# Two transformer blocks in one Trainium2 kernel: who makes the low parts of the weights

## The chip, the core and the metric

The kernel runs on one core of a Trainium2 chip. Its time is the device time of one execution in microseconds, as the median of several runs. Five engines work side by side and meet only through semaphores: TensorE (PE) multiplies, VectorE (DVE), ScalarE (ACT) and GpSimd (POOL) work on tiles elementwise, and SyncE (SP) issues the loads. Each engine works through its own instructions in the order in which they are written, and a wait holds up all that stands behind it.

## The reference

Two decoder blocks on 256 tokens of width 2048, in float32, one after the other:

```
h = x + mixer_block(rms_norm(x, norm_mix_w), w_in, ...)          # HGRN2 scan, 8 heads + banded attention, 16 heads
h = h + square(relu(rms_norm(h, norm_mlp_w) @ w_up)) @ w_down    # d_ff 8192
h = rms_norm(h, norm_final_w)
x = mixer_block_2(h, ...)                                        # gMLP, 8 groups + neighbourhood attention, 16 heads
x = conv_ffn(x, norm_ffn, w_up, conv_k, conv_b, w_down)          # silu(gate) * value, conv of width 3, d_ff 5504
return rms_norm(x, norm_final)
```

Both mixers project the input into heads and gates (w_in), join two branches with w_branch under sigmoid gates, and project back with w_out. Nearly all of the arithmetic is in the large weight products.

## The kernel before, in words

Activations lie transposed, with channels on the partitions and the 256 tokens along the free axis. To keep nearly float32 accuracy with the faster fp32r products, each operand is split into a high part (rounded to fp32r) and a low part (what the rounding left). A product is hi*hi + hi*lo + lo*hi. For this, an activation tile holds its high part in columns 0 to 255 and its low part in columns 256 to 511. The high part of a weight k-tile multiplies all 512 columns (`L401`), its low part only the first 256 (`L403`).

The weights come in 960 blocks, mostly 1024 x 128 (eight k-tiles, 128 x 1024 in SBUF, 512 KB). Every block passes through four hands:

- SyncE loads it into one of five buffers `w_raw` (`L337`), when the low parts of the block four before it are done (`L335`, `L336`).
- ScalarE rounds all 1024 columns into `w_hi` (`round_block`, `L737`), when the data is there and TensorE has used block b.
- VectorE makes columns 0 to 511 of `w_lo` = `w_raw` - `w_hi` (`low_part`, `L1157`), and GpSimd makes columns 512 to 1023 of it with the same instruction (`low_part`, `L1049`), each when `hi_done` says so.
- TensorE waits for both low parts (`L395`, `L396`) and issues the 16 products of the block.

`LEAD` is 4: at step b of a phase the elementwise engines prepare block b+4. The other work is put by hand into the same steps, behind the preparation of the block. `round_block` and `low_part` are the first calls of a step on each engine. Then ScalarE copies the second half of the finished PSUM bank into `cross` (`L742`), VectorE adds the bank's halves (`tile_sum`, `L1163`), which frees the bank (`acc_free`), and multiplies by the row scale (`scaled_tile`, `L1169`, or `L1393`, `L1534`). Most VectorE instructions are followed by a wait for their own semaphore (`mark`, `link`).

The phases: heads1 (8 rounds of 22 blocks: the projections of one scan head and two attention heads, with decay products, softmax and scan between them), branch1, out1, ffn1first, ffn1 (3 rounds of 64 blocks), ffn1last, gmv, heads2 (8 rounds of 16), branch2, out2, ffn2first, ffn2 (2 rounds of 96) and ffn2last. In heads1 the steps 1 to 7 carry the chain of the forget gate: sigmoid and scaling of q (`L1250`), of f (`L1256`, `L1257`), the logarithm on ScalarE (`L816`), its transposition on TensorE (`L461`), the gate of the output (`L1262`) and the low part of the logarithm (`L1265`, `lg_lo`). The steps 8 to 16 carry the decays: `L1280` on VectorE and `L1087` on GpSimd multiply the same exponentials `HS` with q and k, `L1289`, `L1292` and `L1294` mask and reduce their products. In softmax, `L1228` and `L1229` divide by the sums. In the branches `L1352` makes the low part of the merged tile. In ffn2, `L1520` and `L1521` are the convolution's taps.

GpSimd's other work is small: `L1087` in heads1, and the sums of squares for the norms (`L1054`, `L1072`, `L1121`, `L1137`) in the start, out1, ffn1last, out2 and ffn2last. It also sets `ones` in four pieces, each of which counts `lo_pool` up by one, so that the first waits (`CREDIT` = 4) are met.

Of the kernel before, what the change touches and what calls it, by code (L numbers as in the profile page):

```python
# [6 lines left out]
F32 = mybir.dt.float32  # L7
# [29 lines left out]
LEAD = 4  # L37
# [129 lines left out]
def two_blocks(  # L167
# [8 lines left out]
    with ExitStack() as ctx:  # L176
# [87 lines left out]


        landed = [sem(f"landed{s}") for s in range(SLOTS)]
        hi_done, lo_dve, lo_pool, w_used = sem("hi_done"), sem("lo_dve"), sem("lo_pool"), sem("w_used")
        acc_free, cross_ready = sem("acc_free"), sem("cross_ready")
        dve_step, act_step = sem("dve_step"), sem("act_step")
        x_in, c_in, v_in = sem("x_in"), sem("c_in"), sem("v_in")  # L270
# [57 lines left out]
        def _(sp):  # L328
            def load(name, p, i, b):
                kt, ncols = p.shapes.get(b, (KB, P))  # L330
                s = p.slot(b)
                tensor, offset, ap = weight_source(name, i, b)
                freed = p.block(i, b) - REUSE + 1 + CREDIT

                sp.wait_ge(lo_dve, freed)  # L335
                sp.wait_ge(lo_pool, freed)  # L336
                sp.dma_start(w_raw[s][:, 0:kt * ncols].rearrange("p (k n) -> p k n", k=kt),  # L337
                             bass.AP(tensor=tensor, offset=offset, ap=ap)).then_inc(landed[s], 16)

# [46 lines left out]
        def _(pe):  # L386
            def products(p, i, b, bank, X, k0, first, last, nk=KB, col=0, width=P, operand=None):


                s = p.slot(b)  # L390
                hi = w_hi[s][:, 0:nk * width].rearrange("p (k n) -> p k n", k=nk)
                lo = w_lo[s][:, 0:nk * width].rearrange("p (k n) -> p k n", k=nk)
                if col == 0:

                    pe.wait_ge(lo_dve, p.block(i, b) + 1 + CREDIT)  # L395
                    pe.wait_ge(lo_pool, p.block(i, b) + 1 + CREDIT)  # L396
                for k in range(nk):
                    if operand is not None:

                        pe.wait_ge(operand[0], operand[1] + k0 + k + 1)  # L400
                    nc.tensor.matmul(bank[:, :], hi[:, k, col:col + P], X[:, k0 + k, :],  # L401
                                     start=first and k == 0, stop=False, skip_group_check=True)
                    done = nc.tensor.matmul(bank[:, 0:T], lo[:, k, col:col + P], X[:, k0 + k, 0:T],  # L403
                                            start=False, stop=last and k == nk - 1, skip_group_check=True)
                if col + P == width:
                    done.then_inc(w_used, 1)
# [8 lines left out]


            pe.wait_ge(c_in, 16)
            pe.wait_ge(x_in, 16 * NT)
            xn = Gf[:, 0:NT * D].rearrange("p (a n) -> p a n", a=NT)
            banks = [psE, psA]  # L420
# [619 lines left out]

        @block.gpsimd
        def _(pool):
            def low_part(p, i, b):
                c = b + LEAD
                if p is last_phase and c >= p.blocks:
                    return
                s, n = p.slot(c), (p.size(c) if c < p.blocks else BLOCK)
                pool.wait_ge(hi_done, p.block(i, c) + 1)
                nc.gpsimd.tensor_tensor(w_lo[s][:, n // 2:n], w_raw[s][:, n // 2:n], w_hi[s][:, n // 2:n].bitcast(F32),  # L1049
                                        ALU.subtract).then_inc(lo_pool, 1)  # L1050

            def add_square(n):
                pool.wait_ge(sq_ready, n + 1)
                nc.gpsimd.tensor_tensor(sqacc[:, 0, :], sqacc[:, 0, :], sqb[:, 0, :], ALU.add).then_inc(sq_added, 1)  # L1054
# [5 lines left out]
                pool.wait_ge(S("sums_cleared"), cleared[0])  # L1060

            cleared = [0]
            for n in range(CREDIT):
                nc.gpsimd.memset(ones[:, n * 32:(n + 1) * 32], 1.0).then_inc(lo_pool, 1)
            clear_sums()
            for b in range(LEAD):
                pool.wait_ge(hi_done, b + 1)
                nc.gpsimd.tensor_tensor(w_lo[b][:, BLOCK // 2:], w_raw[b][:, BLOCK // 2:], w_hi[b][:, BLOCK // 2:].bitcast(F32),
                                        ALU.subtract).then_inc(lo_pool, 1)
            for j in range(KD):  # L1070
                pool.wait_ge(sq_ready, j + 1)
                nc.gpsimd.tensor_tensor(sqacc[:, 0, :], sqacc[:, 0, :], sqb[:, j % 2, :], ALU.add).then_inc(sq_added, 1)  # L1072
# [2 lines left out]
            p = ph["heads1"]  # L1075
            with pool.Fori(0, p.iters) as i:
                for b in range(p.blocks):
                    low_part(p, i, b)
                    if b in (8, 10, 12, 14):
                        k = (b - 8) // 2  # L1080
                        pool.wait_ge(S("decay_exp"), i * 4 + k + 1)
                        if k == 0:
                            pool.wait_ge(S("g_ready"), i + 1)
                        else:
                            pool.wait_ge(S("pairs_full"), i * 4 + k)
                        kk = wk(1)[:, (k // 2) * P:(k // 2 + 1) * P].rearrange("p (a t) -> p a t", a=1)
                        nc.gpsimd.tensor_tensor(HS[:, 2, :, :], HS[:, 0, :, :], kk.to_broadcast([P, 4, P]), ALU.mult)\  # L1087
                          .then_inc(S("kE_ready"), 1)

            def plain(name):  # L1090
                p = ph[name]
                if p.iters == 1:
                    for b in range(p.blocks):
                        low_part(p, 0, b)
                else:
                    with pool.Fori(0, p.iters) as i:
                        for b in range(p.blocks):
                            low_part(p, i, b)

            def out_projection(name, n0):  # L1100
                p = ph[name]
                with pool.Fori(0, p.iters) as i:
                    for b in range(p.blocks):
                        low_part(p, i, b)
                        if b % 2:
                            add_square(i * 8 + (n0 * KD + b // 2))

            plain("branch1")
            pool.wait_ge(stat_done, 1)
            clear_sums()  # L1110
            out_projection("out1", 1)
            plain("ffn1first")
            plain("ffn1")
            pool.wait_ge(stat_done, 2)
            clear_sums()
            p = ph["ffn1last"]
            for b in range(p.blocks):
                low_part(p, 0, b)
                add_square(2 * KD + b)
                pool.wait_ge(sq2_ready, b + 1)  # L1120
                nc.gpsimd.tensor_tensor(sqacc[:, 1, :], sqacc[:, 1, :], sqb[:, 1, :], ALU.add).then_inc(sq2_added, 1)  # L1121
                pool.wait_ge(sq2_added, b + 1)
            plain("gmv")
            plain("heads2")
            plain("branch2")
            pool.wait_ge(stat_done, 4)
            clear_sums()
            out_projection("out2", 3)
            plain("ffn2first")
            plain("ffn2")  # L1130
            pool.wait_ge(stat_done, 5)
            clear_sums()
            p = ph["ffn2last"]
            for b in range(p.blocks):
                low_part(p, 0, b)
                pool.wait_ge(S("sqf_ready"), b + 1)
                nc.gpsimd.tensor_tensor(sqacc[:, 0, :], sqacc[:, 0, :], wk(6 + b % 2), ALU.add).then_inc(S("sqf_added"), 1)  # L1137
                pool.wait_ge(S("sqf_added"), b + 1)
# [3 lines left out]
        def _(dve):  # L1142
# [8 lines left out]
            def low_part(p, i, b):  # L1151
                c = b + LEAD
                if p is last_phase and c >= p.blocks:
                    return
                s, n = p.slot(c), (p.size(c) if c < p.blocks else BLOCK)
                dve.wait_ge(hi_done, p.block(i, c) + 1)
                V.tensor_tensor(w_lo[s][:, 0:n // 2], w_raw[s][:, 0:n // 2], w_hi[s][:, 0:n // 2].bitcast(F32),  # L1157
                                ALU.subtract).then_inc(lo_dve, 1)

            def tile_sum(p, i, c, b, t, bank, dst):  # L1160
# [16 lines left out]
            dve.wait_ge(acc_free, TILE_CREDIT)  # L1177
            for b in range(LEAD):
                dve.wait_ge(hi_done, b + 1)
                V.tensor_tensor(w_lo[b][:, 0:BLOCK // 2], w_raw[b][:, 0:BLOCK // 2], w_hi[b][:, 0:BLOCK // 2].bitcast(F32),  # L1180
                                ALU.subtract).then_inc(lo_dve, 1)
            banks = (psE, psA)

# [428 lines left out]
```

## Time and profile before

| | |
|---|---|
| runs of the kernel before | 3140.42, 3141.75, 3149.58 us; median 3141.75 |
| span of the profiled execution | 3139.2 us |
| TensorE busy | 2927.3 us, 93% |
| VectorE busy | 2169.0 us, 69% |
| GpSimd busy | 1680.3 us, 54% |
| ScalarE busy | 1515.2 us, 48% |
| DMA | 519.81 MB, mean 166 GB/s |

The profiled execution has its span, from the first to the last instruction, and no time of its own beside the runs; the median of the runs lies 2.5 us above the span. Busy is the time in which an engine has an instruction at work, waits inside of that instruction included. The matmuls' ends are modelled, so a busy TensorE may still be one that runs below its peak; its idle time is better read from the waits. A line number behind L is that of the kernel's text. "A <- B" in a row of waits says that A's engine sat idle until B was done.

### The profile page before, as it was taken

The numbers are of one execution on the slowest core, as the hardware profiler recorded it, in microseconds if no ns is written. First come the engines' busy times: TensorE is split into PE (matmuls) and PEld (weight loads), VectorE is DVE, ScalarE is ACT, GpSimd is POOL, SyncE is SP. The second block draws the span as 40 slices with busy tenths as digits, with TensorE's granted clock in tenths as the row PEclk, the third lists the DMA queues.
The fourth block names the chain that finished last, engine by engine and source line by source line (L and its number), as shares of the span: only waits on it lengthen the run. The fifth ranks groups of instructions, "written<-read, shape, count | busy, mean of one in ns | idle before, by whom it ended". The sixth has DMA issues, their size and how long they took to land.

```text
span 3139.2 us, 53753 instructions
## 1 busy us (share of the span) xinstructions
PE 2927.3 (93%) x16379; PEld 2496.7 (80%) x16379; DVE 2169.0 (69%) x3324; ACT 1515.2 (48%) x2293; POOL 1680.3 (54%) x1105
## 2 busy tenths in 40 slices
PE   5999999989999999999988999899899999999997
PEld 4777777778788888888876777777787788888886
DVE  5777777777568655556577666656747888878885
ACT  5544555556444444444463444445555444444454
POOL 4444445445655666656673445444374455555554
PEclk9999999999999999999999999999999999999998
DMA  5455555545556666666754555565565566666664
GB/s 160 144 146 145 145 145 146 146 140 165 172 173 177 191 190 186 185 183 192 202 148 135 151 155 162 144 163 154 155 188 156 166 182 183 189 177 190 187 182 123
DMA packets 1016035, 519.81 MB, mean 166 GB/s; under 512 B 28980, under 2 KB 1014700, under 8 KB 1015596
## 3 DMA queue, kind: packets, MB, share of 16 engines
q1 hardware_dynamic: 1014032, 513.90, 57.5%
q10 hardware_dynamic: 1820, 3.65, 0.3%
q8 instruction: 93, 1.52, 0.2%
q14 instruction: 90, 0.74, 0.1%
HBM read 515.35 MB, written 2.13 MB: 165 GB/s over the span
## 4 chain that ended last, share of the span: by engine, by line
PE 54%; DVE 27%; issue 9%; ACT 7%; DVEq 1%; DMA 0%; ACTq 0%; SPq 0%; POOL 0%; POOLq 0%
PE acc L401 24%; PE acc L403 12%; DVE w_lo L1157 6%; PE psX L401 5%; PE psT L401 5%; ACT w_hi L737 4%; PE psX L403 2%; PE psT L403 2%; DVE work L1163 2%; DVE work L1534 2%; DVE hT L1362 1%; DVE hT L1361 1%; DVE work L1521 1%; DVE work L1520 1%; DVE HS L1280 1%
## 5 line engine op out<-in xcount | busy, mean ns | idle before, releaser
L1049 POOL TENSOR_TENSOR w_lo<-w_raw,w_hi 128x512 fp32r<-128x512 f32 (+1 forms) x960 | 1548.2, 1625 | 1385.5 <-ACT w_hi L737 1381.5
L1157 DVE TENSOR_TENSOR w_lo<-w_raw,w_hi 128x512 fp32r<-128x512 f32 (+1 forms) x960 | 906.6, 950 | 688.6 <-ACT w_hi L737 634.6
L737 ACT ACTIVATE w_hi<-w_raw 128x1024 fp32r<-128x1024 f32 (+1 forms) x960 | 995.4, 1050 | 601.1 <-PE acc L403 467.4
L401 PE MATMUL acc<-XU,w_hi 128*128 128x512 f32 x3488 | 1256.7, 402 | 26.6 <-DVE work L1163 18.7
L403 PE MATMUL acc<-XU,w_lo 128*128 128x256 f32 x3488 | 983.6, 282 | 0.0
L401 PEld LDWEIGHTS acc<-XU,w_hi 128*128 128x128 f32 x3488 | 662.0, 190 | 195.7 <-DVE w_lo L1157 18.5
L401 PE MATMUL acc<-XY,w_hi 128*128 128x512 f32 x2112 | 768.6, 405 | 44.6 <-DVE work L1163 18.4
L403 PEld LDWEIGHTS acc<-XU,w_lo 128*128 128x128 f32 x3488 | 665.5, 191 | 1.1
L403 PE MATMUL acc<-XY,w_lo 128*128 128x256 f32 x2112 | 598.9, 284 | 0.0
L401 PEld LDWEIGHTS acc<-XY,w_hi 128*128 128x128 f32 x2112 | 404.0, 191 | 151.1 <-DVE w_lo L1157 23.6
L403 PEld LDWEIGHTS acc<-XY,w_lo 128*128 128x128 f32 x2112 | 407.2, 193 | 0.1
L401 PE MATMUL psT<-XY,w_hi 128*128 128x512 f32 x632 | 226.4, 398 | 14.2 <-issue 9.4
L401 PE MATMUL psX<-XY,w_hi 128*128 128x512 f32 x632 | 225.6, 397 | 2.0 <-DVE work L1163 1.6
L403 PE MATMUL psT<-XY,w_lo 128*128 128x256 f32 x632 | 177.3, 281 | 0.0
L403 PE MATMUL psX<-XY,w_lo 128*128 128x256 f32 x632 | 177.2, 280 | 0.0
L401 PEld LDWEIGHTS psT<-XY,w_hi 128*128 128x128 f32 x632 | 118.6, 188 | 45.5 <-issue 11.7
L1002 ACT ACTIVATE work<-work,convc 128x256 f32<-128x256 f32 x86 | 51.8, 603 | 190.8 <-DVE work L1534 190.7
L401 PEld LDWEIGHTS psX<-XY,w_hi 128*128 128x128 f32 x632 | 118.6, 188 | 31.3 <-DVE w_lo L1157 1.7
L401 PE MATMUL psX<-XU,w_hi 128*128 128x512 f32 x352 | 125.5, 396 | 1.9 <-DVE work L1163 1.1
L401 PE MATMUL psT<-XU,w_hi 128*128 128x512 f32 x352 | 125.1, 395 | 0.4 <-POOL w_lo L1049 0.4
L1163 DVE TENSOR_TENSOR work<-acc,cross 128x256 f32<-128x256 f32 x290 | 120.7, 416 | 5.5 <-ACT cross L742 5.2
L403 PEld LDWEIGHTS psT<-XY,w_lo 128*128 128x128 f32 x632 | 119.4, 189 | 0.0
(250 smaller groups left out, 2993.5 us busy)
## 6 DMA issues: line engine op xcount, KB each, us to landing
w_raw<-in_w_in SPq DMA_DIRECT2D x320, 512.0 KB, 3.9
w_raw<-in_w_up SPq DMA_DIRECT2D x300, 512.0 KB, 4.4
w_raw<-in_w_down SPq DMA_DIRECT2D x208, 512.0 KB, 4.3
w_raw<-in_w_out SPq DMA_DIRECT2D x64, 512.0 KB, 3.9
w_raw<-in_w_branch SPq DMA_DIRECT2D x32, 512.0 KB, 3.8
w_raw<-in_w_branch_a SPq DMA_DIRECT2D x16, 512.0 KB, 3.8
w_raw<-in_w_branch_b SPq DMA_DIRECT2D x16, 512.0 KB, 3.8
bias<-in_rel_bias SPq DMA_DIRECT2D x8, 384.0 KB, 5.1
```

What stands on the lines that cost most here:

```text
L401: nc.tensor.matmul(bank[:, :], hi[:, k, col:col + P], X[:, k0 + k, :], start=first and k == 0, stop=False, skip_group_check=True)
L403: done = nc.tensor.matmul(bank[:, 0:T], lo[:, k, col:col + P], X[:, k0 + k, 0:T], start=False, stop=last and k == nk - 1, skip_group_check ...
L737: act.activation(w_hi[s][:, 0:n], w_raw[s][:, 0:n], ACT.Copy).then_inc(hi_done, 1)
L1002: act.activation(wk(2 + u.value), work[:, u.value, 0:T], ACT.Identity, scale=convc[:, 0, ds(ch, 1)], bias=convc[:, 3, ds(ch, 1)]).then_inc ...
L1049: nc.gpsimd.tensor_tensor(w_lo[s][:, n // 2:n], w_raw[s][:, n // 2:n], w_hi[s][:, n // 2:n].bitcast(F32), ALU.subtract).then_inc(lo_pool, 1)
L1157: V.tensor_tensor(w_lo[s][:, 0:n // 2], w_raw[s][:, 0:n // 2], w_hi[s][:, 0:n // 2].bitcast(F32), ALU.subtract).then_inc(lo_dve, 1)
L1163: mark(V.tensor_tensor(dst, bank[:, 0:T], cross[:, c % 2, :], ALU.add), acc_free, p.tile(i, t) + 1 + TILE_CREDIT)
L1280: mark(V.tensor_tensor(HS[:, 1, :, :], HS[:, 0, :, :], q.to_broadcast([P, 4, P]), ALU.mult), S("qE_ready"), i * 4 + k + 1)
L1361: link(V.tensor_tensor(h, bank[:, 0:T].rearrange("p (a t) -> p a t", a=1), h, ALU.add))
L1362: mark(V.tensor_tensor(h, bank[:, T:2 * T].rearrange("p (a t) -> p a t", a=1), h, ALU.add), acc_free, p.tile(i, t) + 1 + TILE_CREDIT)
L1520: link(V.scalar_tensor_tensor(y, z, convc[:, 1, ds(ch, 1)], y, ALU.mult, ALU.add))
L1534: mark(V.tensor_tensor(z, z, rs[:, :], ALU.mult), S("conv_z"), (made(name, i, s.group) + s.t) * 2 + s.value + 1)
```

## The change

The low part of a block is made by one VectorE instruction on all 1024 columns. GpSimd's half, its semaphore `lo_pool` and all waits for it are gone; GpSimd keeps its other work. `ones` is set by one instruction, and TensorE waits for it once, at its start.

```diff
@@ SyncE, load
                 sp.wait_ge(lo_dve, freed)
-                sp.wait_ge(lo_pool, freed)
@@ TensorE, products
                     pe.wait_ge(lo_dve, p.block(i, b) + 1 + CREDIT)
-                    pe.wait_ge(lo_pool, p.block(i, b) + 1 + CREDIT)
@@ TensorE, start
             pe.wait_ge(c_in, 16)
+            pe.wait_ge(S("ones_set"), 1)
             pe.wait_ge(x_in, 16 * NT)
@@ GpSimd
-            def low_part(p, i, b):
-                c = b + LEAD
-                if p is last_phase and c >= p.blocks:
-                    return
-                s, n = p.slot(c), (p.size(c) if c < p.blocks else BLOCK)
-                pool.wait_ge(hi_done, p.block(i, c) + 1)
-                nc.gpsimd.tensor_tensor(w_lo[s][:, n // 2:n], w_raw[s][:, n // 2:n], w_hi[s][:, n // 2:n].bitcast(F32),
-                                        ALU.subtract).then_inc(lo_pool, 1)
...
-            for n in range(CREDIT):
-                nc.gpsimd.memset(ones[:, n * 32:(n + 1) * 32], 1.0).then_inc(lo_pool, 1)
+            nc.gpsimd.memset(ones[:, :], 1.0).then_inc(S("ones_set"), 1)
...
@@ VectorE, low_part
                 dve.wait_ge(hi_done, p.block(i, c) + 1)
-                V.tensor_tensor(w_lo[s][:, 0:n // 2], w_raw[s][:, 0:n // 2], w_hi[s][:, 0:n // 2].bitcast(F32),
+                V.tensor_tensor(w_lo[s][:, 0:n], w_raw[s][:, 0:n], w_hi[s][:, 0:n].bitcast(F32),
                                 ALU.subtract).then_inc(lo_dve, 1)
@@ VectorE, start
-                V.tensor_tensor(w_lo[b][:, 0:BLOCK // 2], w_raw[b][:, 0:BLOCK // 2], w_hi[b][:, 0:BLOCK // 2].bitcast(F32),
+                V.tensor_tensor(w_lo[b][:, :], w_raw[b][:, :], w_hi[b][:, :].bitcast(F32),
                                 ALU.subtract).then_inc(lo_dve, 1)
```

In GpSimd's program the calls of `low_part` go with it, also in the phases in which it did nothing else.

## Rows read from the trace of the kernel before

In rows 2 and 10 the columns are: the stretch and its length; busy us of PE, PEld, DVE, ACT and POOL, each with its count; TensorE's granted clock; the DMA share; GB/s.

**Rows 1.** The chain that ended last: share of the span by engine.
```profile
PE 54%; DVE 27%; issue 9%; ACT 7%; DVEq 1%; DMA 0%; ACTq 0%; SPq 0%; POOL 0%; POOLq 0%
```
**Rows 2.** Stretches: heads1, branch1, ffn1first, ffn1, ffn1last, gmv, heads2, ffn2first, ffn2.
```profile
43.40:697.80 654.40, 603.38 (x3426) 508.84 (x3425) 471.10 (x673) 329.10 (x521) 316.45 (x208) 0.99 0.50 144
697.80:802.10 104.30, 93.57 (x514) 79.63 (x513) 79.13 (x129) 65.26 (x121) 51.45 (x32) 0.98 0.55 159
...
893.60:1038.50 144.90, 137.79 (x772) 119.59 (x771) 111.53 (x143) 63.34 (x86) 71.54 (x50) 0.98 0.60 174
1038.50:1577.20 538.70, 536.43 (x3075) 469.99 (x3074) 319.23 (x577) 231.33 (x288) 338.03 (x193) 1.00 0.67 190
1577.20:1629.80 52.60, 45.99 (x258) 38.94 (x256) 48.10 (x64) 33.65 (x59) 48.76 (x45) 0.97 0.53 155
1629.80:1709.30 79.50, 61.89 (x300) 49.62 (x301) 55.22 (x74) 33.58 (x50) 30.85 (x23) 0.89 0.48 131
1709.30:2162.70 453.40, 418.40 (x2306) 344.59 (x2304) 282.50 (x428) 208.90 (x329) 213.22 (x127) 0.98 0.56 152
...
2358.80:2517.80 159.00, 144.60 (x803) 122.29 (x803) 125.62 (x187) 78.41 (x119) 73.59 (x53) 1.00 0.55 159
2517.80:3072.70 554.90, 545.64 (x3074) 471.79 (x3072) 449.33 (x652) 272.26 (x391) 307.89 (x193) 1.00 0.65 186
```
**Rows 3.** VectorE: a group (busy, mean ns), two lines (ns minimum/median/maximum).
```profile
L1157 DVE TENSOR_TENSOR w_lo<-w_raw,w_hi 128x512 fp32r<-128x512 f32 x952 | 898.9, 950 | 688.3 <-ACT w_hi L737 634.6 <-issue 7.3 <-DVE hT L1362 1.7
...
L1157 DVE TENSOR_TENSOR w_lo<-w_raw,w_hi x960: 557/693/1836, 50.5 to 3114.3; 128x512 fp32r<-128x512 f32 x192
...
L1534 DVE TENSOR_TENSOR work<-work,rs x86: 426/1065/1073, 2372.1 to 3067.5; 128x256 f32<-128x256 f32 x86
```
**Rows 4.** GpSimd's groups: its half of the low parts.
```profile
L1049 POOL TENSOR_TENSOR w_lo<-w_raw,w_hi 128x512 fp32r<-128x512 f32 x952 | 1539.9, 1630 | 1359.7 <-ACT w_hi L737 1355.7
```
**Rows 5.** Order of time in one round of heads1, VectorE: start, duration.
```profile
302.83 1.52 DVE L1250 SCALAR_TENSOR_TENSOR work<-work 128x256 f32<-128x256 f32 x1
304.47 1.58 DVE L1157 TENSOR_TENSOR w_lo<-w_raw,w_hi 128x512 fp32r<-128x512 f32 x1
...
308.95 1.38 DVE L1256 TENSOR_SCALAR work<-work,small 128x256 f32<-128x256 f32 x1
...
317.07 1.50 DVE L1262 SCALAR_TENSOR_TENSOR work<-work,small 128x256 f32<-128x256 f32 x1
...
320.18 0.41 DVE L1265 TENSOR_TENSOR lg_lo<-psT,lg_hi 128x256 fp32r<-128x256 f32 x1
```
**Rows 6.** VectorE's widest instruction, 1024 columns: ns minimum/median/maximum.
```profile
L1561 DVE TENSOR_SCALAR G<-G,small x2: 746/749/752, 3130.9 to 3131.5; 128x1024 f32<-128x1024 f32 x2
```
**Rows 7.** Waits of the weight loads in heads1: total, times, longest.
```profile
PEld psT L461 <- ACT work L816: 24.7, 8, 3.4
```
**Rows 8.** Order of time in heads1: the decay multiplies of VectorE and GpSimd.
```profile
346.47 1.78 DVE L1280 TENSOR_TENSOR HS<-HS,work 128x512 f32<-128x512 f32 x1
...
347.66 1.55 POOL L1087 TENSOR_TENSOR HS<-HS,work 128x512 f32<-128x512 f32 x1
```
**Rows 9.** heads2: a wait of the weight loads, and a group of the softmax.
```profile
PEld acc L401 <- DVE w_lo L1157: 14.0, 8, 1.8
...
L1228 DVE TENSOR_SCALAR probs<-probs,soft 128x256 f32<-128x256 f32 x24 | 27.7, 1153 | 0.9
```
**Rows 10.** The stretch behind the softmax's wait in one round of heads2.
```profile
1927.00:1933.00 6.00, 5.98 (x25) 4.60 (x25) 3.19 (x6) 1.06 (x1) 0.81 (x2) 0.72 0.82 216
```
**Rows 11.** Order of time in branch1's second round.
```profile
789.89 1.25 DVE L1352 TENSOR_TENSOR XU<-work,XU 128x256 f32 x1 [0.18 <-DVE work L1347]
```
**Rows 12.** Waits of the weight loads in gmv.
```profile
PEld acc L401 <- DVE G L1163: 11.5, 5, 6.7
```
**Rows 13.** Order of time in ffn2: one period of six blocks, begin and end.
```profile
2600.43 1.07 DVE L1534 TENSOR_TENSOR work<-work,rs 128x256 f32<-128x256 f32 x1
...
2617.39 1.07 DVE L1534 TENSOR_TENSOR work<-work,rs 128x256 f32<-128x256 f32 x1
```

More of the change, by code:

```diff
@@ L266, in two_blocks @@
         landed = [sem(f"landed{s}") for s in range(SLOTS)]
-        hi_done, lo_dve, lo_pool, w_used = sem("hi_done"), sem("lo_dve"), sem("lo_pool"), sem("w_used")
+        hi_done, lo_dve, w_used = sem("hi_done"), sem("lo_dve"), sem("w_used")
         acc_free, cross_ready = sem("acc_free"), sem("cross_ready")
@@ L1062, in _ @@
             cleared = [0]
-            for n in range(CREDIT):
-                nc.gpsimd.memset(ones[:, n * 32:(n + 1) * 32], 1.0).then_inc(lo_pool, 1)
+            nc.gpsimd.memset(ones[:, :], 1.0).then_inc(S("ones_set"), 1)
             clear_sums()
[L1066 to L1069, printed above, removed]
             for j in range(KD):
@@ L1077, in _ @@
                 for b in range(p.blocks):
-                    low_part(p, i, b)
                     if b in (8, 10, 12, 14):
@@ L1088, in _ @@
                           .then_inc(S("kE_ready"), 1)
[L1090 to L1098, printed above, removed]
             def out_projection(name, n0):
@@ L1103, in out_projection @@
                     for b in range(p.blocks):
-                        low_part(p, i, b)
                         if b % 2:
                             add_square(i * 8 + (n0 * KD + b // 2))
-            plain("branch1")
             pool.wait_ge(stat_done, 1)
@@ L1111, in _ @@
             out_projection("out1", 1)
-            plain("ffn1first")
-            plain("ffn1")
             pool.wait_ge(stat_done, 2)
@@ L1117, in _ @@
             for b in range(p.blocks):
-                low_part(p, 0, b)
                 add_square(2 * KD + b)
@@ L1122, in _ @@
                 pool.wait_ge(sq2_added, b + 1)
-            plain("gmv")
-            plain("heads2")
-            plain("branch2")
             pool.wait_ge(stat_done, 4)
@@ L1128, in _ @@
             out_projection("out2", 3)
-            plain("ffn2first")
-            plain("ffn2")
             pool.wait_ge(stat_done, 5)
@@ L1134, in _ @@
             for b in range(p.blocks):
-                low_part(p, 0, b)
                 pool.wait_ge(S("sqf_ready"), b + 1)
```

## The prediction

> **What bounds the kernel now.** I read the chain of waits first, then the stretches, then the groups of instructions, and at last the order of time inside one head. The chain shows TensorE with 54% of the span and VectorE with 27% [rows 1]. So TensorE sets the pace, and where it does not, VectorE's chain does. The stretches say where [rows 2]. TensorE multiplies 960 weight blocks of eight k-tiles. In ffn1 a block costs 538.7 / 192 = 2.81 us and the engine is busy all the time; I take that as the floor. Everywhere else a block costs more: heads1 3.72 (654.4 / 176), branch1 3.26, ffn1first 3.02, ffn1last 3.29, gmv 4.97, heads2 3.54, ffn2first 3.18, ffn2 2.89. Part of the excess is the small products between blocks. The rest is waiting on VectorE, mostly on what comes out of a long chain ScalarE, VectorE, ScalarE.
>
> Why those chains are long stands in the groups. VectorE's half of a low part takes 0.95 us in the mean and 0.69 in the median; `L1534`, the same operation on 256 columns, takes 0.43 at its shortest and 1.07 in its median [rows 3]. GpSimd's half takes 1.63 us in the mean [rows 4]. In order of time: VectorE's half runs first, GpSimd starts just behind it, and the next VectorE instruction on SBUF alone takes 1.52 (`L1250`), 1.38 (`L1256`) or 1.50 (`L1262`), while `L1265`, which reads PSUM, takes 0.41 [rows 5]. So the two engines shut each other out for whole instructions. The Trainium skill has this in SBUF — State Buffer, "Who interferes with whom": a VectorE instruction with two SBUF inputs and a GpSimd instruction that reads SBUF exclude each other for the whole of whichever started first. The trace agrees (1.07 against 0.43).
>
> **The price of the new low part.** No instruction of that form and width is in the trace. From below, the only VectorE instruction on 1024 columns takes 0.75, with one input [rows 6]. From above, two halves in a row are 2 x 0.69 = 1.38 by the undisturbed half, or 2 x 0.95 = 1.90 by the mean. I take the line through the undisturbed 256 and 512 columns, 0.43 and 0.69 [rows 3]: 0.26 to 0.27 for each 256, hence 0.69 + 2 x 0.267 = 1.23. So each low part costs VectorE 1.23 - 0.69 = 0.54 more than a free half, 0.28 more than the mean half (960 x 0.28 = 269 us busy), and w_lo is complete after 1.23 instead of the 1.75 that GpSimd's slower half usually needs. What is freed is the 0.6 to 1.1 us on each instruction that was shut out. Cases run from a VectorE chain with one low part and one shut-out instruction (gain 0.54 lost, 0.64 to 1.1 won) to one with three low parts and none (1.6 lost). The sum is made stretch by stretch.
>
> Edits at nothing: one memset of `ones` for four and TensorE's wait for it lie under the loads of x (the first transposes wait for these anyway; uncovered, below 0.5 us). SyncE's loads and TensorE's blocks lose a wait on GpSimd; they now hang on VectorE's alone, which comes 0.5 earlier where VectorE is on time. Four blocks of lead (11 us) cover the rest.
>
> **heads1, 8 rounds, -20 us.** The gate of the first half is `psT L461`, 24.7 us of waiting, and behind it lg_lo, which ends at 320.59 [rows 7, 5]. I replay the chain with 1.23 and 0.42, and 0.35 for one-input ones on 256 columns (an estimate from the 0.75 for 1024). Link hq to hf: low +0.54, `L1250` -1.10, low 1.58 to 1.23 -0.35: -0.9. Link to Ln: two lows +1.08, `L1256` -1.03, and its successor `L1257`, shut out the same way, -0.91: -0.9. Link to lg_lo: +0.54 -1.08 (`L1262`) -0.33: -0.9. The two lows at the head of the round give up to 0.8 more, of which I count 0.3: -3.0 a round. Second half (b 10 to 17): eight low parts, six short ones +0.6 each, two long ones -0.4 each, against three `L1280` (1.78 to 0.69 in one [rows 8], 1.50 in the others), `L1294` twice (-1.0, -0.5) and `L1228` (-0.7). If VectorE goes first at `L1280` this is -0.6; if GpSimd's multiply `L1087` does [rows 8] (about 1.1 alone), VectorE waits for it and it is +1.1. It will often be asked for while VectorE's longer low part still runs, so I take +0.5. The same section of the skill says that whoever starts first decides, which speaks against the change here; by it alone this half is +1.1 and heads1 -15. Sum: 8 x (-3.0 + 0.5) = -20, bounds -29 and -10.
>
> **heads2, 8 rounds, -23 us.** No GpSimd work is left here. TensorE waits 14.0 us, 1.75 a round, where the row names w_lo; the instruction behind is the sum of tile 5 that frees the bank [rows 9], and before it for the softmax (1.5). On that chain stand three free lows (+0.54 each), `L1476` (1.53 to 0.56), four `L1228`/`L1229` (1.15 in the mean [rows 9], to 0.35; -3.2) and a low of 1.55 to 1.23. That is 1.6 - 1.0 - 3.2 - 0.3 = -2.9 of chain; of the 3.2 that TensorE waits there I give back 2.3 a round, 18 in all. The wait drops the granted clock: 0.72 in the 6 us behind one [rows 10], a good half of them at the lower level of 1.2 GHz; a block takes 4.3 instead of 2.7. In five of eight rounds I see this; -5 for it. Bounds -28 and -10.
>
> **branch1 and branch2 with the start of out1 and out2, -13.** A pair of blocks costs VectorE 6.40 in the second round against TensorE's 5.6. Of this `L1352` is shut out, 1.25 [rows 11]. New: +0.61 for the short low, -0.83, -0.26: 5.9. Over 16 pairs VectorE falls behind by about 5 instead of 13 us, less than the lead for most of the way; the waits at b 8 to 14 (2.9) go and the last one (5.9) shrinks to about 3. -6 each, -1 for the clock. Bounds -4 and -20.
>
> **ffn1first, -9.** VectorE's cycle of two blocks is 6.27; new 5.3, below TensorE's 5.55. The stretch lies 144.9 - 48 x 2.81 = 10 above the floor [rows 2], nearly all of it waiting on this cycle; 9 of it goes. Bounds -5 and -10.
>
> **ffn1last and gmv, -11.** VectorE's cycle in ffn1last is 3.40 a block (a shut-out low of 1.67); new 2.65 alone, up to 3.24 with GpSimd's square sums between. The end of the chain, on which gmv's first sums hang, comes 4.5 earlier. In gmv the cycle of a pair falls from 6.8 to 5.9: -5.5 of the 11.5 [rows 12], and 1 at the end. Bounds -5 and -18.
>
> **ffn2first -5, ffn2 -2, ffn1 and the ends 0.** In ffn2first's mixed part VectorE and ScalarE are in step, 15.0 a round of five blocks. Deltas: +0.61 +0.60 for lows, -0.50 -0.46 for long ones, -0.64 for `L1534`: 14.6, 8 rounds, -3.3; 2 more at its head. In ffn2 the period is 2617.39 - 2600.43 = 16.96 for six blocks [rows 13]. VectorE's own chain there comes to 16.96 now and 16.6 after, so no new bound appears, but the margin is only 0.3. ffn1's VectorE is busy 1.7 of 2.8 us a block and 2.1 after; hidden. In ffn2last the low stands before the output copies: +1.
>
> Sum: -20 -23 -13 -9 -11 -5 -2 = -83, by rounding with the +1. From the profiled 3139.2 this gives 3056; the median of the runs (3141.75) is 2.5 above the span, so **3059 us**. The terms' bounds give 3010 to 3105.
>
> **Rivals.**
> *The lockstep eats it (3104).* Chains cross ScalarE, whose round (1.05) and copies stay, and each new low stands at the head of a step, before the sum that frees the bank. Then heads1 gives 8, heads2 10, the branches 7, ffn1first 7, gmv 6, the rest nothing: -38. For it: VectorE's total busy time stays about what it is (269 us more for the lows, about 320 us less elsewhere). Against: the gates I name all stand behind a shut-out instruction.
> *More than counted (3029).* A block in ffn2 costs 2.89 and in ffn1 2.81 [rows 2] with TensorE nearly always busy in both; if the slow manner goes with VectorE's lateness, 192 x 0.08 = 15 us go there and as much in the other stretches. For: it is in the stretches with the fuller VectorE. Against: one of ffn1's three rounds has it too.
> *Slower: VectorE becomes the bound (3337).* If the long durations are not GpSimd's doing, a full low part costs 2 x 0.95 = 1.90, 0.67 above my price. Then ffn2's period is 16.6 + 6 x 0.67 = 20.6, +3.7 on 32 periods, +118 against now; heads1 and heads2 lose half of 304 x 0.67, 102; the branches 43, ffn2first 27. With the -83 that is about +195, some of the rest counted in. It decides from a low part of 1.4 us on, where the loss on all of these equals 83. Against: the PSUM reader at 0.41 amid its slow neighbours [rows 5]. Nor does the change fail to do what it says: the row of GpSimd's w_lo must vanish.
>
> **How the numbers follow.** Forecast 0.60 (its own range 3030 to 3092), lockstep 0.20, more 0.12, slower 0.07, no change 0.01. The range 3015 to 3125 holds the first three nearly whole. A difference under 0.3% can't be told from none here. Faster by more 0.88 (the first three less 0.04 for the lockstep case's weak end), within 0.05, slower 0.07.
>
> **What would show it.** `L1534`, `L1250`, `L1169` at 0.42 to 0.43 throughout and the new w_lo group at 1.23 with little spread; VectorE busy within 80 us of 2169. The wait of `psT L461` for ScalarE from 3.1 a round to below 1; `psT L531` in heads2 without a wait; heads1's round 81.8 to about 79.3, heads2's 56.7 to about 53.8; ffn1 at 538 unchanged; ffn2 within 5 us. The forecast is wrong if a low part takes over 1.4, if ffn2's period rises above 17, or if heads1's round stays, which would put the gate on ScalarE.

## The result, and the profile after

The changed kernel is faster. Four runs took 3024.90 to 3035.66 us, median 3031.61, against a median of 3145.45 for four runs of the kernel before. The ratio is 0.9631, with a 95% interval from 0.9611 to 0.9651. On another chip it was 0.9652 (0.9627 to 0.9676). The forecast was 3059 and the range 3015 to 3125, so mechanism and side were right and the size was short: 83 us forecast, 114 measured between the medians, 105 between the two spans. The measured time lies at the edge of the forecast's own range (3030 to 3092) and nearer to the 3029 of the rival "more than counted" than to 3059; what became of that rival stands below.

The profiled execution has a span of 3033.9 us. This is the page's busy time, each engine with its share and its count, and the chain of waits by engine, which answers to [rows 1]:

```profile
PE 2901.6 (96%) x16379; PEld 2480.3 (82%) x16379; DVE 2170.2 (72%) x3324; ACT 1524.8 (50%) x2293; POOL 133.9 (4%) x138
...
PE 65%; DVE 17%; issue 9%; ACT 7%; DVEq 1%; DMA 0%; ACTq 0%; SPq 0%; POOL 0%; POOLq 0%
```

VectorE took over GpSimd's half of the low parts and is busy for as long as before (2170.2 for 2169.0 us). Its share of the chain fell from 27% to 17%. The groups and lines of VectorE show why. They answer to [rows 3] and to the first row of [rows 5]; the first row gives busy time and mean ns, the others minimum, median and maximum:

```profile
L1120 DVE TENSOR_TENSOR w_lo<-w_raw,w_hi 128x1024 fp32r<-128x1024 f32 x952 | 1164.8, 1228 | 591.9 <-ACT w_hi L736 531.0 <-issue 17.6 <-DVE hT L1325 1.2
...
L1497 DVE TENSOR_TENSOR work<-work,rs x86: 424/426/429, 2288.8 to 2961.2; 128x256 f32<-128x256 f32 x86
...
L1213 DVE SCALAR_TENSOR_TENSOR work<-work x8: 418/418/422, 56.2 to 606.5; 128x256 f32<-128x256 f32 x8
...
L1243 DVE TENSOR_TENSOR HS<-HS,work x32: 691/1582/1591, 74.9 to 647.3; 128x512 f32<-128x512 f32 x32
```

The whole low part takes 1.228 us, where the line through two widths gave 1.23. The row scale of ffn2 (`L1534`, now `L1497`) had a median of 1065 ns and now has 426, with a maximum of 429. `L1243`, the old `L1280`, is still shut out, 24 of 32 times and 21 us in all: GpSimd's multiply is the one large thing GpSimd kept beside it. Beside GpSimd's sums of squares at the start and in ffn1last, `L1149` takes 753 ns in the mean for 473 at its shortest, `L1330` 720 for 484, and six low parts are longer too, about 11 us together.

The stretches, in the order of [rows 2] and with its columns: heads1, branch1, ffn1first, ffn1, ffn1last, gmv, heads2, ffn2first, ffn2.

```profile
42.50:672.10 629.60, 594.95 (x3425) 503.22 (x3424) 456.81 (x673) 331.25 (x521) 42.23 (x33) 1.00 0.53 150
672.10:772.80 100.70, 91.72 (x514) 79.32 (x513) 77.45 (x129) 66.28 (x122) 0.00 (x0) 0.97 0.56 164
...
865.40:1002.20 136.80, 136.30 (x773) 118.02 (x772) 96.05 (x144) 63.76 (x86) 1.26 (x2) 1.00 0.64 186
1002.20:1547.10 544.90, 543.23 (x3074) 470.54 (x3073) 385.25 (x577) 230.79 (x288) 0.00 (x0) 1.00 0.65 188
1547.10:1595.50 48.40, 45.48 (x259) 39.21 (x257) 45.41 (x65) 34.04 (x60) 33.98 (x28) 1.00 0.60 175
1595.50:1665.60 70.10, 61.56 (x300) 50.56 (x301) 45.31 (x74) 34.22 (x50) 4.62 (x5) 0.88 0.52 141
1665.60:2088.40 422.80, 409.16 (x2306) 338.86 (x2304) 270.07 (x428) 208.08 (x329) 0.00 (x0) 1.00 0.60 164
...
2276.50:2423.50 147.00, 143.18 (x804) 122.62 (x803) 115.33 (x189) 78.78 (x120) 1.27 (x2) 1.00 0.59 172
2423.50:2965.50 542.00, 538.32 (x3074) 467.95 (x3072) 423.21 (x650) 277.58 (x391) 0.00 (x0) 1.00 0.66 190
```

heads2 gives most (453.4 to 422.8), then heads1 (654.4 to 629.6), ffn1last with gmv (132.1 to 118.5), ffn2 (554.9 to 542.0) and ffn2first (159.0 to 147.0). One of these stretches got longer: ffn1, 538.7 to 544.9, though TensorE is busy in nearly all of it in both traces (536.4 and 543.2 us).

The waits of TensorE's weight loads in heads1 answer to [rows 7]: total, times, longest.

```profile
PEld psA L495 <- DVE HS L1252: 25.9, 8, 3.3
PEld psE L472 <- DVE lg_lo L1228: 10.9, 8, 1.4
PEld psT L460 <- ACT work L815: 5.3, 7, 1.1
```

The wait for the logarithm fell from 24.7 to 5.3. The wait for the masked products (`HS`) rose from 16.5 to 25.9 and is now the largest.

### The profile page after: what moved, and what is told of

Read it like the earlier page. It is cut to its first block, busy times and chain, and to the rows that moved or that the text cites. A ratio compares the mean times of both kernels' runs of the same rounds, so it can differ in the third digit from the quotient of the medians.

```text
span 3033.9 us, 50114 instructions
## 1 busy us (share of the span) xinstructions
PE 2901.6 (96%) x16379; PEld 2480.3 (82%) x16379; DVE 2170.2 (72%) x3324; ACT 1524.8 (50%) x2293; POOL 133.9 (4%) x138
## 3 DMA queue, kind: packets, MB, share of 16 engines
q8 instruction: 90, 1.47, 0.2%
## 4 chain that ended last, share of the span: by engine, by line
PE 65%; DVE 17%; issue 9%; ACT 7%; DVEq 1%; DMA 0%; ACTq 0%; SPq 0%; POOL 0%; POOLq 0%
PE acc L399 29%; PE acc L401 14%; PE psT L399 6%; PE psX L399 6%; DVE w_lo L1120 5%; ACT w_hi L736 4%; PE psX L401 3%; PE psT L401 3%; DVE work L1126 1%; DVE probs L1184 1%; DVE HS L1243 1%; ACT probs L782 1%; DVE soft L1185 1%; DVE work L1132 1%; DVE HS L1252 1%
## 5 line engine op out<-in xcount | busy, mean ns | idle before, releaser
L1120 DVE TENSOR_TENSOR w_lo<-w_raw,w_hi 128x1024 fp32r<-128x1024 f32 (+1 forms) x960 | 1171.9, 1226 | 592.1 <-ACT w_hi L736 531.0
L399 PE MATMUL acc<-XU,w_hi 128*128 128x512 f32 x3488 | 1243.7, 399 | 6.7 <-DVE work L1126 6.0
L401 PEld LDWEIGHTS psX<-XY,w_lo 128*128 128x128 f32 x632 | 119.2, 189 | 0.0
L1044 POOL TENSOR_TENSOR sqacc<-sqacc,sqb 128x256 f32<-128x256 f32 x48 | 44.7, 932 | 1562.5 <-ACT sqb L878 1562.0
```

The costliest lines, as they stand in the source:

```text
L1120: V.tensor_tensor(w_lo[s][:, 0:n], w_raw[s][:, 0:n], w_hi[s][:, 0:n].bitcast(F32), ALU.subtract).then_inc(lo_dve, 1)
```

## The experiments

Three questions were open. How much is the shutting out worth, and how much of it does VectorE's longer instruction give back? Does the longer instruction cost because of its length or because of its place? And what moved ffn1 and ffn2? Each version was timed beside the kernel before, which took 3148.3 us in the median beside the first four, 3146.9 beside the next four and 3148.7 beside the last, on another chip.

**The same kernel once more.**

> The changed kernel itself once more, on the chip of the next ones. Theory A (two manners of TensorE): in a stretch without a stall TensorE keeps one of two cadences, 346.7 or 352 ns for a pair of products, and which one is decided anew at each stall; then ffn1 (545.0 us, all slow in the first trace) and ffn2 (542.0, first round slow, second fast) can differ by up to 10 us each from trace to trace of the same program, while heads1 and heads2 stay within 5. Rival B: the cadence belongs to the program; then the same rounds are slow again and all stretches agree within 2 us.

Measured: 3039.34 us, ratio 0.9652. The two traces of one program disagree where theory A said. These windows have the same clock (1.00) and no idle TensorE, first in the trace after, then in the second trace:

```profile
1190.00:1360.00 170.00, 170.00 (x964) 147.51 (x963) 121.55 (x181) 72.00 (x90) 0.00 (x0) 1.00 0.64 185
2700.00:2900.00 200.00, 200.00 (x1156) 174.83 (x1155) 156.03 (x241) 103.30 (x145) 0.00 (x0) 1.00 0.66 190
```

```profile
1190.00:1360.00 170.00, 170.00 (x982) 149.90 (x982) 121.74 (x182) 73.06 (x91) 0.00 (x0) 1.00 0.66 188
2700.00:2900.00 200.00, 200.00 (x1133) 173.49 (x1132) 153.51 (x236) 101.19 (x142) 0.00 (x0) 1.00 0.65 187
```

In 170 us TensorE issued 964 products in one trace and 982 in the other, and in ffn2 it is the other way round (1156 and 1133). That is 1.9 to 2.0%. Worked out from the starts of the products, a pair takes 346.7 or 353.3 ns in the mean of a round (waits left out), and a whole round of ffn1 or ffn2 keeps one of the two. ffn1 took 545.0 and 541.9, ffn2 542.0 and 546.8; heads1 629.6 and 632.2. So the cadence is not the program's, and B falls. That it is decided anew at each stall, as A has it, no run shows. In the second trace block 19 of two rounds of heads1 ran at the lower level of the clock (1.2 for 2.4 GHz) and took 5.3 and 5.0 us for 3.9; in the first trace none did.

**Half of each low part left out.** GpSimd's half is gone and VectorE does not take it over; those columns stay at zero from the start.

```diff
-                V.tensor_tensor(w_lo[s][:, 0:n], w_raw[s][:, 0:n], w_hi[s][:, 0:n].bitcast(F32),
+                V.tensor_tensor(w_lo[s][:, 0:n // 2], w_raw[s][:, 0:n // 2], w_hi[s][:, 0:n // 2].bitcast(F32),
... the same at VectorE's start, and GpSimd clears the other columns once
```

> Leaves out the second half of each low part (its columns are zero from the start), so neither engine makes it: VectorE does 0.69 a block, GpSimd nothing. Theory A: the gain of the change is the shutting out that went (about -140 to -150 us by itself), of which VectorE's longer low part (1.23 for 0.69) gives back 30 to 45: about 2990 us, ratio 0.952, most of the difference to the change in heads1 and heads2, which have 8 and 3 low parts on the chains that gate TensorE. Rival B (VectorE's own work costs nothing, it is all hidden): 3030 as the change itself, ratio 0.963.

Measured: 2934.05 us, ratio 0.9319 (0.9299 to 0.9340). Against the kernel before this is nearly the shutting out alone, with VectorE's work unchanged: 3148.3 - 2934.1 = 214 us. TensorE's own waits for GpSimd's half, which went with it, were 3.7 us in all in the trace before, of which this is the largest row:

```profile
PE acc L401 <- POOL w_lo L1049: 2.6, 3, 1.9
```

Against the change on the same chip it is 3039.3 - 2934.1 = 105 us, which is what the longer low part gives back. Theory A had the right signs and both sizes too small, B falls. TensorE has hardly an idle moment in heads1 (589.2 us) and heads2 (407.5). The zeros are not what makes it fast there: a later version with all columns made has the same two lengths.

**Two halves on VectorE.**

```diff
-                V.tensor_tensor(w_lo[s][:, 0:n], w_raw[s][:, 0:n], w_hi[s][:, 0:n].bitcast(F32),
-                                ALU.subtract).then_inc(lo_dve, 1)
+                V.tensor_tensor(w_lo[s][:, 0:n // 2], w_raw[s][:, 0:n // 2], w_hi[s][:, 0:n // 2].bitcast(F32), ALU.subtract)
+                V.tensor_tensor(w_lo[s][:, n // 2:n], w_raw[s][:, n // 2:n], w_hi[s][:, n // 2:n].bitcast(F32),
+                                ALU.subtract).then_inc(lo_dve, 1)
```

> The change with VectorE making the low part in two instructions of half a block. Theory A: 2 x 0.69 = 1.38 for 1.23 in trains of two; VectorE busy +140 us, and 0.15 more for each low part on a gating chain: heads1 +8, heads2 +4, branches and gmv +4, in all about 3047, ratio 0.969. Rival B (the width of the instruction is what brings the gain): above 3080.

Measured: 3069.17 us, ratio 0.9729 (0.9686 to 0.9772), between the two theories: 30 us above the change on this chip, where A has 15 and B 48 or more (3047 and 3080 against 3031.6). The halves take 0.692 and 0.701 us. The four runs range from 3047.9 to 3081.4 us, and the trace is that of the slowest. In it the loss is largest in heads1, 655.9 for 629.6: 3.3 us a round. Its waits for the logarithm, lg_lo and `HS` grew by 0.3, 0.1 and 0.4 us a round, and in all eight rounds block 19 ran at the lower level of the clock and took 5.4 to 6.3 us for 3.9; that costs 2.2 a round, two thirds of the loss. The second and third of these blocks:

```profile
191.50:198.00 6.50, 5.75 (x19) 4.98 (x20) 5.92 (x13) 1.20 (x2) 0.00 (x0) 0.50 0.37 102
273.50:280.00 6.50, 5.74 (x19) 4.96 (x20) 5.92 (x13) 1.22 (x2) 0.00 (x0) 0.50 0.36 105
```

What puts the clock down there is not settled, and two rounds of the change's second trace show it too. So one instruction for two is worth about 30 us here in the median, from 9 to 42 by the run; in the traced run a good part of it comes by way of the clock.

**GpSimd kept beside the whole low part.** GpSimd makes its half once more, behind VectorE's.

```diff
 # from the kernel before; VectorE makes w_lo[s][:, 0:n]
-                pool.wait_ge(hi_done, p.block(i, c) + 1)
+                pool.wait_ge(lo_dve, p.block(i, c) + 1 + CREDIT)
                 nc.gpsimd.tensor_tensor(w_lo[s][:, n // 2:n], w_raw[s][:, n // 2:n], w_hi[s][:, n // 2:n].bitcast(F32),
... the same for the first four blocks
```

> VectorE makes the whole low part as in the change, and GpSimd makes its half once more behind it, so its instruction follows VectorE's as in the kernel before and can shut out the next one on SBUF. Theory A: the shut-out waits come back (0.6 to 1.1 us on the instruction behind each low part) on top of 1.23: ffn2's period of six blocks rises from 16.7 to about 20, heads1 and heads2 by 8 and 4 us a round against the change, the sum about 3300, slower than before; L1534's kind is back at 1.07 to 1.7. Rival B (the waits of VectorE had another cause than GpSimd's reads): within 1% of the change.

Measured: 3402.10 us, ratio 1.0813 (1.0789 to 1.0837). A's direction holds, its size was 100 us too small. The groups of VectorE and GpSimd in this version (busy, mean ns):

```profile
L1157 DVE TENSOR_TENSOR w_lo<-w_raw,w_hi 128x1024 fp32r<-128x1024 f32 x952 | 1300.7, 1378 | 396.5 <-ACT w_hi L737 320.1 <-issue 14.8 <-DVE hT L1362 1.4
L1534 DVE TENSOR_TENSOR work<-work,rs 128x256 f32<-128x256 f32 x86 | 98.9, 1150 | 2.9
...
L1049 POOL TENSOR_TENSOR w_lo<-w_raw,w_hi 128x512 fp32r<-128x512 f32 x952 | 1413.1, 1490 | 1746.1 <-DVE w_lo L1157 1744.1
```

`L1534` is back at 1.15, from 0.43 where GpSimd makes no low parts. Order of time in ffn2 shows one after the other what GpSimd's instruction does to those with SBUF inputs (1.38, 1.28) and to those that read PSUM (0.42):

```profile
2561.01 1.38 DVE L1521 SCALAR_TENSOR_TENSOR work<-work,convc 128x256 f32<-128x256 f32 x1
2563.89 1.23 DVE L1157 TENSOR_TENSOR w_lo<-w_raw,w_hi 128x1024 fp32r<-128x1024 f32 x1 [1.50 <-ACT w_hi L737]
2565.03 0.42 DVE L1163 TENSOR_TENSOR work<-acc,cross 128x256 f32<-128x256 f32 x1
2565.49 1.28 DVE L1534 TENSOR_TENSOR work<-work,rs 128x256 f32<-128x256 f32 x1
```

Four versions now stand in a square. TensorE waits for GpSimd's late half in the last one, so its corner holds that too.

| us, ratio | VectorE makes half (0.69) | VectorE makes all (1.23) |
|---|---|---|
| GpSimd makes a half | 3148.3, 1 | 3402.1, 1.0813 |
| GpSimd makes none | 2934.1, 0.9319 | 3039.3, 0.9652 |

GpSimd's half costs 214 us beside a half and 363 beside the whole. VectorE's second half costs 105 without GpSimd and 254 with it. The change goes over the diagonal: -214 + 105 = -109.

**The low part last in the step, heads1 and heads2.**

```diff
                 for b in range(p.blocks):
-                    low_part(p, i, b)
                     t = b // 2
...
                         low_of_attention(1, i, XY)
+                    low_part(p, i, b)
```

> The change with VectorE's low part at the end of each step instead of its head, in heads1 and heads2 only. Leaving half of each low part out brought 40 us in heads1 and 15 in heads2 against the change. Theory A (a low part costs because it stands ahead of the tile sum and the chain's multiplies in the same step, not because VectorE is full): the waits of TensorE for lg_lo, HS and the keys shrink from 5.2 us a heads1 round and 2.1 a heads2 round to below 2 and 1, heads1 about 605 us for 630, heads2 about 412 for 423, in all near 3000, ratio 0.953. Rival B (VectorE's total work in the chain counts, wherever it stands, because it is without a gap there): within 8 us of the change, ratio 0.964.

Measured: 2973.60 us, ratio 0.9445 (0.9429 to 0.9460). heads1 588.6 and heads2 405.8 us, what the version with half of the work left out had (589.2 and 407.5). So the same instructions on the same engine cost nothing that the trace shows there once they stand behind the chain's own. B falls, and A was too cautious: the waits for the logarithm, lg_lo and `HS` are gone, not smaller. The largest wait of the weight loads left in that stretch is that of the start:

```profile
PEld psS L412 <- POOL sqacc L1057: 4.7, 1, 4.7
```

**GpSimd's multiply on VectorE.**

```diff
... GpSimd's part in heads1 is gone
+                        kk = wk(1)[:, (k // 2) * P:(k // 2 + 1) * P].rearrange("p (a t) -> p a t", a=1)
+                        mark(V.tensor_tensor(HS[:, 2, :, :], HS[:, 0, :, :], kk.to_broadcast([P, 4, P]), ALU.mult),
+                             S("kE_ready"), i * 4 + k + 1)
```

> The change with GpSimd's multiply of the decays with k (1.10 us, and 1.58 for VectorE's own multiply behind it where 0.69 is free) made by VectorE. Theory A (GpSimd goes first and shuts VectorE out for about 0.9 a time): VectorE's pair costs 2 x 0.69 = 1.38 for 1.58, three times on the chain to HS, so the 3.2 us wait of each heads1 round shrinks by some 0.5: -2 to -6 us in all. Rival B (the added 0.69 is on the chain in full): heads1 +15 to +20 us.

Measured: 3028.39 us, ratio 0.9617 (0.9593 to 0.9642), not to be told from the change. heads1 took 631.5 us for 629.6. B's 15 to 20 us did not come. A's 2 to 6 can't be seen in the time, but they are in the waits: that for `HS` fell from 25.9 to 23.3, and a round of heads1 with block 19 at the full clock takes 78.1 to 78.2 us (the first apart) for 78.4 to 78.6. In three rounds block 19 ran at the lower level, which takes it away again. VectorE does twice 0.69 where it did 0.69 and waited 0.89.

```profile
PEld psA L495 <- DVE HS L1241: 23.3, 8, 3.0
```

**The low part last everywhere, and with the multiply on VectorE.**

```diff
 # in branches, out_projection, ffn1, gmv, heads2 and ffn2 alike
-                        low_part(p, i, b)
...
+                        low_part(p, i, b)
```

> The low part at the end of VectorE's step in every phase. Theory A: as the version in heads1 and heads2 alone, and besides gmv -5, ffn2first -5, ffn2last -2, ffn1last -2, branches -3: about 2985 us, ratio 0.949. Rival B: in steps that wait for ScalarE or TensorE at their end the low part of block b+4 comes too late, TensorE waits for w_lo, and the stretches with a full VectorE (branches, ffn2first) get longer by 5 to 10 us each.

> Both: low part last in every phase and the multiply with k on VectorE. With theory A of both, 2 to 6 us below the version with the low part last; with rival B of the multiply 15 above it. If the chain to HS no longer gates, the multiply changes nothing (within 3 us).

Measured: 2943.45 us, ratio 0.9344 (0.9328 to 0.9361), and with the multiply 2952.67, 0.9369 (0.9344 to 0.9395). The first is the fastest complete version, 3% below the change and 42 us below A's 2985. Beyond heads1 and heads2 it took gmv from 70.2 to 64.7, ffn2first from 147.0 to 140.5 and ffn2last from 68.3 to 61.8 us. No stretch got longer by more than the cadence does, so B falls here too. The multiply brings nothing that can be told apart: the medians differ by 9 us, the intervals overlap, and heads1 takes 589.2 for 587.6. The stretch of heads1 shows TensorE busy in 587.18 of 587.60 us:

```profile
42.50:630.10 587.60, 587.18 (x3420) 502.87 (x3421) 442.39 (x676) 333.62 (x520) 48.17 (x34) 1.00 0.57 160
```

**The kernel before with VectorE's half last in the step.**

> The kernel before, both engines making their halves, with VectorE's half moved to the end of its step in every phase (GpSimd's stays at the head of its own). Theory A (the place on VectorE takes the low part off the chains, but GpSimd's half still shuts out the multiply behind each tile sum): about half of what the move brought to the changed kernel, near 3090 us, ratio 0.982, L1534's kind still near 1.0 us. Rival B (the place alone was the matter, who makes the half is not): as the changed kernel with the low part last, 2943, ratio 0.935.

Measured: 3008.60 us, ratio 0.9554 (0.9538 to 0.9570), between A and B. The place alone is worth 140 us in the kernel before, more than the change itself, and more than the 96 us that the same move brought the changed kernel (3039.3 to 2943.5), where A had expected half of it. heads1 and heads2 give 101 of the 133 us between the spans (654.4 to 599.9 and 453.4 to 406.7), and TensorE no longer waits for the logarithm, lg_lo or `HS` there. GpSimd's half on top costs 3008.6 - 2943.5 = 65 us, a third of the 214 it cost with the low part first. The groups of this version (busy, mean ns) show that it still shuts VectorE out, `L1534`'s kind (here `L1533`) somewhat less, 0.77 in the mean for 0.99, where A had it near 1.0. By the waits, less of that lies on a chain that TensorE waits for:

```profile
L1157 DVE TENSOR_TENSOR w_lo<-w_raw,w_hi 128x512 fp32r<-128x512 f32 x952 | 902.9, 956 | 189.4 <-ACT w_hi L737 100.5 <-issue 6.6 <-DVE hT L1362 0.9
L1533 DVE TENSOR_TENSOR work<-work,rs 128x256 f32<-128x256 f32 x86 | 66.1, 769 | 3.0
```

## Why the prediction was right, step by step

| term, us | forecast | span of trace after - before |
|---|---|---|
| heads1 | -20 | -24.8 |
| heads2 | -23 | -30.6 |
| branches with out1, out2 | -13 | -10.4 |
| ffn1first | -9 | -8.1 |
| ffn1last and gmv | -11 | -13.7 |
| ffn2first | -5 | -12.1 |
| ffn2 | -2 | -12.9 |
| ffn1 | 0 | +6.4 |
| start, ffn2last | +1 | +0.9 |
| sum | -83 (rounded) | -105 |

- **The cause.** GpSimd and VectorE shut each other out for whole instructions. Shown: with GpSimd's half gone, `L1534`'s kind goes from a mean of 987 ns (median 1065) to 426 ns; with its half back, to a mean of 1150.
- **The price of the low part**, 1.23: measured 1.228. The 0.35 for one-input instructions on 256 columns holds too: those of the softmax (`L1228`, `L1229` before) take 0.353 after.
- **Nothing gained in VectorE's busy time.** Forecast within 80 us of 2169, measured 2170.2.
- **heads1, first half.** The chain to lg_lo was to get 3.0 us shorter a round. The wait at the logarithm fell from 3.1 to 0.7 a round. At lg_lo 1.4 stays, about as before, since TensorE comes there sooner by as much.
- **heads1, second half.** Here the forecast weighed who goes first at the multiplies and took a middle value. In all 32 cases GpSimd asked while VectorE's long low part was still running. In 24 it still held VectorE's multiply up; in the first of each round's four it was through in time. The order of time in one round, VectorE's rows first:

```profile
314.87 1.23 DVE L1120 TENSOR_TENSOR w_lo<-w_raw,w_hi 128x1024 fp32r<-128x1024 f32 x1 [0.97 <-ACT w_hi L736]
316.01 1.58 DVE L1243 TENSOR_TENSOR HS<-HS,work 128x512 f32<-128x512 f32 x1
...
315.82 1.23 POOL L1071 TENSOR_TENSOR HS<-HS,work 128x512 f32<-128x512 f32 x1 [5.44 <-ACT HS L825]
```

  GpSimd asks at 315.82, while the low part runs, and VectorE's multiply, which starts its 1.58 behind the low part at 316.01, waits for it. The wait at `HS` rose from 2.1 to 3.2 us a round, the +1.1 of the forecast's upper bound. That the number agrees is in part luck: the parts listed for this half add up to -2.1 and not to the -0.6 given for VectorE going first, and with the 0.89 that GpSimd's multiply costs each of three they come to +0.6. The Trainium skill's rule in SBUF — State Buffer, "Who interferes with whom", that the one who starts first decides, came true to its sign. The version with half of each low part left out shows it in both directions, again VectorE's rows first:

```profile
73.41 1.47 DVE L1246 TENSOR_TENSOR HS<-HS,work 128x512 f32<-128x512 f32 x1
...
78.37 0.69 DVE L1246 TENSOR_TENSOR HS<-HS,work 128x512 f32<-128x512 f32 x1 [0.20 <-ACT HS L825]
...
73.23 1.10 POOL L1073 TENSOR_TENSOR HS<-HS,work 128x512 f32<-128x512 f32 x1 [31.42 <-ACT HS L825]
78.41 1.60 POOL L1073 TENSOR_TENSOR HS<-HS,work 128x512 f32<-128x512 f32 x1 [4.08 <-ACT HS L825]
```

  Where GpSimd starts 0.18 us sooner, VectorE's multiply takes 1.47; where VectorE starts 0.04 sooner, it takes 0.69 and GpSimd's 1.60. The whole term was still larger than forecast, because TensorE's idle time at the gate behind it, the freeing of the bank at block 20, went from 0.7 us a round to none instead of moving.
- **heads2.** -2.3 us a round and 5 for the clock were forecast. The stretch's granted clock rose from 0.98 to 1.00 and no block of it ran at the lower level any more, so the clock's part was about 8 us (five blocks took 5.9 for 4.4). The chain's part was -2.8 a round: the two waits that the forecast names fell by 2.4 (14.0 and 11.9 us in all to 6.6 and none), and one that it does not name, for `L1169` at the first transposition, by 0.55 (15.9 to 11.5 in all).
- **ffn2, a term that was mis-sized.** The forecast compared the period of six blocks (16.96 to 16.6) and found no new bound, which holds. But it left out the waits at the seams. Before, TensorE waited 2.0 and 0.6 at the first blocks, 2.2 at the end of the first round and 5.4 at the end of the second for the last hidden tile, because VectorE was behind; after, 1.1, 0.8 and 2.7. That is some 6 of the 12.9, with 1.6 for a block at the lower clock. The cadence gave 5 (96 blocks of 8 pairs at 6.6 ns less): before, both rounds were slow, after, one. This part is luck.
- **ffn2first.** The forecast took 15.0 to 14.6 for a round of five blocks in the mixed part and -2 at its head; 12.1 came. The head gave its 2 (37.1 to 35.0). The round fell to 14.1, because the forecast counted +0.6 for a short low part that costs +0.54 and -0.5 for long ones that gave -0.7 and -0.6; and the first two rounds, which it took at 15.0, had cost 16.2 and 15.8 before and took 13.4 and 14.0 after. TensorE's idle time fell by 10.6 in this stretch. The version with the low part last takes another 6.5.
- **ffn1.** 0 forecast, +6.4 measured. The cadence accounts for all of it: two more of the three rounds were slow, 128 blocks at 353.3 instead of 346.7 ns for each of eight pairs, 6.8 us. It is no effect of the change: the second trace has one fast round.
- **The range.** The bounds given for the terms add up to a gain of 112 us at the most, hence 3030, not the 3010 of the text; the two spans differ by 105.
- **The rivals.** The lockstep case held that a low part at the head of each step eats the gain. It eats half of it: 105 of 214. The time did not come out at its 3104, but its mechanism was real, and it named what the better version moves. "More than counted" had nearly the right time (3029 for 3031.6) for a reason that did not hold: it let the slow manner go away with VectorE's lateness, 15 us in ffn2 and as much elsewhere. The cadence gave 5 in ffn2 and took 7 in ffn1, and one program has both. What was more than counted came out of the waits. The slower case had VectorE's long durations from another cause; the square above rules it out.

What stays open is what sets TensorE's cadence, and why the clock falls behind some waits and not behind others.

## What to carry to other kernels

Before an engine is relieved, read whether its helper delays it: an instruction whose median is far above its minimum, at one shape, next to siblings that read PSUM and are not delayed, says that it does; whether the helper takes away more than it gives has to be measured. Here a helper that made half of the work cost 214 us and saved 105. Work with a lead of several blocks is worth trying behind the step's own chain and not at its head: that move alone was worth 140 us in the kernel before, and with the change it reaches 2943 us.

## What the runs showed of the hardware

- TensorE has two cadences at one granted clock of 1.00: 346.7 and 353.3 ns for a pair of products of 512 and 256 columns. They last for whole rounds of ffn1 (64 blocks) and ffn2 (96), in every version where TensorE is not stopped, and differ between two traces of one program. Over the 956 blocks of 8 pairs this is at most some 50 us, an estimate from the 6.6 ns, and it is why stretches without any wait moved by 5 us. In the kernel before, both are seen in ffn1, the first window in its second round and the second in its third:

```profile
1250.00:1350.00 100.00, 100.00 (x568) 86.76 (x567) 58.28 (x107) 42.97 (x53) 63.46 (x36) 1.00 0.65 186
1400.00:1500.00 100.00, 100.00 (x579) 88.19 (x578) 58.27 (x107) 42.53 (x54) 61.57 (x36) 1.00 0.67 188
```

- 0.17 us more for each low part, in two instructions for one, cost 30 us in the median: short waits in series, and, in the traced run, a block at the lower clock (1.2 for 2.4 GHz) in each round of heads1.
- The same wait does not always bring the lower clock: in heads2 of the kernel before, TensorE stood idle for 1.53 to 1.55 us in front of the same block in every round, and the block fell to the lower level in five of eight (5.93 us for 4.40); after the change the idle time there is 0.45 to 0.66 and none falls.
